# Forming two of the four weight sums of a seven-product matmul by an accumulating transfer instead of on VectorE

## The reference

```python
h2 = rmsnorm(x, norm2_g[l])                                        # (1, 256, 2048)
x = x + jnp.square(jax.nn.relu(h2 @ w_mlp_in[l])) @ w_mlp_out[l]   # 2048 -> 8192 -> 2048
```

## Time and profile before

| | us |
|---|---|
| median of three runs | 2813.29 |
| the three runs | 2812.1, 2817.95, 2813.29 |
| the profiled execution, its time | 2816.21 |
| its span (first to last instruction) | 2814.5 |
| TensorE busy | 2791.1 |
| VectorE busy | 2227.4 |
| ScalarE busy | 1489.3 |
| GpSimd busy | 2.0 |
| share of the 16 DMA engines taken by SyncE's queue | 68.8% |

### The profile page before, as it was taken

The page is one execution under the profiler, slowest core; times in us unless marked ns, Lnnn a source line. Parts: engine busy times, 40 slices in busy tenths (PEclk is TensorE's granted clock), DMA queues, the critical chain, the costliest instruction groups (busy, mean ns, idle before and its releaser), DMA issues.

```text
span 2814.5 us, 33866 instructions
## 1 busy us (share of the span) xinstructions
PE 2791.1 (99%) x13102; PEld 2300.4 (82%) x13102; DVE 2227.4 (79%) x2487; ACT 1489.3 (53%) x1674; POOL 2.0 (0%) x7
## 2 busy tenths in 40 slices
PE   9999999999999999999999999999999999999998
PEld 7888878888887888888888888888888788888887
DVE  6697855556778999999967678877667999999986
ACT  6644446544455555555556444444455555555654
POOL 0000000000000000000000000000000000000000
PEclk9999999999999999999999999999999999999999
DMA  9576656666866677767677767667676767677774
GB/s 313 160 222 201 204 160 211 195 195 198 257 210 212 219 235 243 245 212 239 223 243 218 223 199 215 200 206 224 209 219 208 243 215 239 219 242 226 246 233 166
DMA packets 371808, 615.42 MB, mean 219 GB/s; under 512 B 22976, under 2 KB 96320, under 8 KB 371008
## 3 DMA queue, kind: packets, MB, share of 16 engines
q1 hardware_dynamic: 371216, 612.94, 68.8%
q10 hardware_dynamic: 432, 0.32, 0.0%
HBM read 575.69 MB, written 2.10 MB: 205 GB/s over the span
## 4 chain that ended last, share of the span: by engine, by line
PE 83%; DVE 8%; DMA 5%; ACT 2%; issue 2%; SPq 1%; DVEq 0%; ACTq 0%
PE ACC L864 67%; PE TB L870 8%; PE ACC L870 6%; DVE WL L1609 2%; DMA RAW<-in_w_mlp_in_dram 2%; DMA RAW<-in_w_up_dram 2%; DMA RAW<-in_w_down_dram 1%; DVE FG L1622 1%; ACT WH L1136 1%; DVE FG L1624 1%; DVE FG L1626 1%; DVE X L2121 0%; DVE HT L2094 0%; SPq L758 0%; DVE TWL L1633 0%
## 5 line engine op out<-in xcount | busy, mean ns | idle before, releaser
L1136 ACT ACTIVATE WH<-RAW 128x1024 fp32r<-128x1024 f32 (+1 forms) x1023 | 1027.8, 1020 | 1016.4 <-PE ACC L864 619.1
L1609 DVE TENSOR_TENSOR WL<-RAW,WH 128x1024 fp32r<-128x1024 f32 (+1 forms) x1023 | 1185.6, 1172 | 405.5 <-ACT WH L1136 402.5
L864 PE MATMUL ACC<-WH,XTH 128*128 128x512 f32 (+1 forms) x1692 | 658.1, 389 | 0.4 <-DVE XTL L1683 0.4
L864 PE MATMUL ACC<-WL,XTH 128*128 128x512 f32 (+1 forms) x1692 | 655.1, 387 | 0.0
L864 PE MATMUL ACC<-WH,XTL 128*128 128x512 f32 (+1 forms) x1692 | 655.1, 387 | 0.0
L864 PEld LDWEIGHTS ACC<-WH,XTH 128*128 128x128 f32 x1692 | 317.8, 188 | 66.8 <-DVE XTL L1683 0.8
L864 PEld LDWEIGHTS ACC<-WH,XTL 128*128 128x128 f32 x1692 | 317.7, 188 | 65.1
L864 PEld LDWEIGHTS ACC<-WL,XTH 128*128 128x128 f32 x1692 | 317.8, 188 | 63.6
L864 PE MATMUL ACC<-WH,YAH 128*128 128x512 f32 x864 | 336.4, 389 | 0.0
L864 PE MATMUL ACC<-WL,YAH 128*128 128x512 f32 x864 | 336.1, 389 | 0.0
L864 PE MATMUL ACC<-WH,YAL 128*128 128x512 f32 x864 | 336.1, 389 | 0.0
(11 more groups left out here) (383 smaller groups left out, 3146.6 us busy)
## 6 DMA issues: line engine op xcount, KB each, us to landing
RAW<-in_w_in_dram SPq DMA_DIRECT2D x255, 512.0 KB, 4.5
RAW<-in_w_mlp_out_dram SPq DMA_DIRECT2D x128, 512.0 KB, 5.0
RAW<-in_w_down_dram SPq DMA_DIRECT2D x128, 512.0 KB, 5.1
RAW<-in_w_mlp_in_dram SPq DMA_DIRECT2D x116, 512.0 KB, 4.6
RAW<-in_w_up_dram SPq DMA_DIRECT2D x116, 512.0 KB, 4.5
RAW<-in_w_gate_dram SPq DMA_DIRECT2D x96, 512.0 KB, 4.5
YT<-HT SPq DMA_DIRECT2D x208, 128.0 KB, 3.2
RAW<-in_w_branch_dram SPq DMA_DIRECT2D x48, 512.0 KB, 4.1
```

The source lines that it names most:

```text
L864: ins = e.matmul(ACC[:, 2 * (b % 2) + half, 0:n], p[:, k, xs], q[:, t, 0:n], start=(k == 0 and m == 0), stop=(k == nk - 1 and m == 2))
L1136: e.activation(WH[u % NSPL][:, ts, 0:n], RAW[u % NRAW][:, ts, 0:n], ACT.Copy).then_inc(hi, 1)
L1609: e.tensor_tensor(l, r, h, ALU.subtract).then_inc(lo, 1)
```

## The change

For the quads made ahead (24 in the run), the first VectorE instruction of three (L1622, 128 x 1024: T1 and T3 at once) goes. Instead GpSimd issues one transfer with an add: it reads the two tiles of the pair's second block again from HBM (512 KB) and adds them to slots 0 and 2 of `FG`, where SyncE has just loaded the tiles of the first block's upper row and the second block's upper row. GpSimd waits for the load first (`ld_sum`), and VectorE now waits for the add (`add_sum`) and then makes T2 and T4 with one instruction of 512 columns each.

A transfer can add and not subtract, so all quads use sums with other signs: in `weight_sums` every `subtract` becomes `add`. To make up for it `x_sums` swaps operands and turns one add and one subtract round, and `product_sums` uses two `tensor_tensor` subtracts and two `scalar_tensor_tensor` instead of four `tensor_tensor` adds. The counts that `t_sum` reaches come from a table, since a quad made ahead now counts two and not three.

The positions change too. The sum of the first quad moves from h - 15 to h - 14, its high part from h - 14 to h - 13, its low part from h - 11 and h - 10 to h - 12 and h - 11. The second quad's load moves from unit h - 3 to h - 4, its sum from h - 6 to h - 5, its high part from h - 5 to h - 4, its low part from h - 4 and h - 3 to h - 3 and h - 2.

```diff
+    SUMMED = {}
+    for rec in sorted({rec for rec, m in SEVEN.values()}, key=lambda rec: rec.q):
+        SUMMED[rec.q] = SUMMED.get(rec.q - 1, 0) + (2 if rec.ahead else 3)
...
-            at("ahead_sum", h - 15)
-            at("ahead_hi", h - 14)
-            at("ahead_lo", h - 11, 2)
-            at("ahead_sum", h - 6)
-            at("ahead_hi", h - 5)
-            at("ahead_lo", h - 4, 2)
-            AHEAD_LOAD[h - 13], AHEAD_LOAD[h - 3] = AHEAD_OF[n, 0], AHEAD_OF[n, 1]
+            at("ahead_add", h - 16)
+            at("ahead_sum", h - 14)
+            at("ahead_hi", h - 13)
+            at("ahead_lo", h - 12, 2)
+            at("ahead_add", h - 8)
+            at("ahead_sum", h - 5)
+            at("ahead_hi", h - 4)
+            at("ahead_lo", h - 3, 2)
+            AHEAD_LOAD[h - 13], AHEAD_LOAD[h - 4] = AHEAD_OF[n, 0], AHEAD_OF[n, 1]
...
             if rec.ahead:
-                b11_12, b12_22, b21, b22 = tr[:, 0:4:2, :], tr[:, 2:4, :], tr[:, 1, :], tr[:, 3, :]
-                e.wait_ge(ld_sum, 32 * LOADED[rec.q])
+                b21, b22 = tr[:, 1, :], tr[:, 3, :]
+                e.wait_ge(add_sum, 16 * LOADED[rec.q])
...
-            e.tensor_tensor(tr[:, T1:T3 + 1:T3 - T1, :], b12_22, b11_12, ALU.subtract).then_inc(t_sum, 1)
-            e.wait_ge(t_sum, 3 * rec.q + 1)
-            e.tensor_tensor(tr[:, T2, :], b22, tr[:, T1, :], ALU.subtract).then_inc(t_sum, 1)
-            e.wait_ge(t_sum, 3 * rec.q + 2)
-            e.tensor_tensor(tr[:, T4, :], b21, tr[:, T2, :], ALU.subtract).then_inc(t_sum, 1)
+            if not rec.ahead:
+                e.tensor_tensor(tr[:, T1:T3 + 1:T3 - T1, :], b12_22, b11_12, ALU.add).then_inc(t_sum, 1)
+                e.wait_ge(t_sum, SUMMED[rec.q] - 2)
+            e.tensor_tensor(tr[:, T2, :], b22, tr[:, T1, :], ALU.add).then_inc(t_sum, 1)
+            e.wait_ge(t_sum, SUMMED[rec.q] - 1)
+            e.tensor_tensor(tr[:, T4, :], b21, tr[:, T2, :], ALU.add).then_inc(t_sum, 1)
...
-            e.tensor_tensor(sx[:, S_1], AX[:, :, 0, 1, :], AX[:, :, 1, 1, :], ALU.add).then_inc(xs, 1)
-            e.tensor_tensor(sx[:, S_3], sx[:, S_A], AX[:, :, 0, 1, :], ALU.subtract).then_inc(xs, 1)
+            e.tensor_tensor(sx[:, S_1], AX[:, :, 1, 1, :], AX[:, :, 0, 1, :], ALU.subtract).then_inc(xs, 1)
+            e.tensor_tensor(sx[:, S_3], AX[:, :, 0, 1, :], sx[:, S_A], ALU.subtract).then_inc(xs, 1)
...
-                e.tensor_tensor(h12, h11, acc_bank(b0, 1), ALU.add).then_inc(mid, 1)
+                e.tensor_tensor(h12, acc_bank(b0, 1), h11, ALU.subtract).then_inc(mid, 1)
                 e.wait_ge(mid, 2 * n + 1)
-                e.tensor_tensor(h21, h12, acc_bank(b0 + 1, 1), ALU.add).then_inc(acc[b0 % 2], 1)
+                e.scalar_tensor_tensor(out=h21, in0=h12, scalar=-1.0, in1=acc_bank(b0 + 1, 1), op0=ALU.mult, op1=ALU.subtract
+                                       ).then_inc(acc[b0 % 2], 1)
...
+        def sum_add():
+            for k, rec in enumerate(AHEAD_OF.values()):
+                w, _, c0, n = plan[PAIR[rec.u][1] + 1]
+                rows = w[2 * rec.i * P:(2 * rec.i + 2) * P, c0:c0 + n].rearrange("(g t j) n -> j (g t) n", g=4, t=2)
+                e.wait_ge(ld_sum, 32 * k + 32)
+                e.dma_start(TR[rec.buf[1]][:, 0:4:2, :], rows, accum_op=ALU.add).then_inc(add_sum, 16)
+                yield
+
+        tasks = {"gm_tril": gm_tril, "ahead_add": sum_add, "block1_end": pad}
```

More of the change, by code:

```diff
@@ L189, in build @@
     ld_x0 = [sem(f"ld_x0_{k}") for k in range(8)]
-    ld_sum = sem("ld_sum_tiles")
+    ld_sum, add_sum = sem("ld_sum_tiles"), sem("sum_tiles_added")
     ld_gb = [sem(f"ld_gate_bias{i}") for i in range(2)]
@@ L772, in _ @@
                 if u - NRAW in SEVEN and not SEVEN[u - NRAW][0].ahead:
-                    e.wait_ge(t_sum, 3 * SEVEN[u - NRAW][0].q + 3)
+                    e.wait_ge(t_sum, SUMMED[SEVEN[u - NRAW][0].q])
             if u == 0:
@@ L1140, in sums_high @@
             sums_free(e, rec)
-            e.wait_ge(t_sum, 3 * rec.q + 2)
+            e.wait_ge(t_sum, SUMMED[rec.q] - 1)
             e.activation(parts[0][:, T_PARTS[0], :], tr[:, T_PARTS[0], :], ACT.Copy).then_inc(t_hi, 1)
-            e.wait_ge(t_sum, 3 * rec.q + 3)
+            e.wait_ge(t_sum, SUMMED[rec.q])
             e.activation(parts[0][:, T_PARTS[1], :], tr[:, T_PARTS[1], :], ACT.Copy).then_inc(t_hi, 1)
@@ L2158, in x_sums @@
             e.wait_ge(xs, m + NI + 2)
-            e.tensor_tensor(sx[:, S_1], AX[:, :, 0, 1, :], AX[:, :, 1, 1, :], ALU.add).then_inc(xs, 1)
-            e.tensor_tensor(sx[:, S_3], sx[:, S_A], AX[:, :, 0, 1, :], ALU.subtract).then_inc(xs, 1)
+            e.tensor_tensor(sx[:, S_1], AX[:, :, 1, 1, :], AX[:, :, 0, 1, :], ALU.subtract).then_inc(xs, 1)
+            e.tensor_tensor(sx[:, S_3], AX[:, :, 0, 1, :], sx[:, S_A], ALU.subtract).then_inc(xs, 1)
             yield
             e.wait_ge(xs, m + NI + 3)
-            e.tensor_tensor(sx[:, S_2], sx[:, S_1], sx[:, S_A], ALU.subtract).then_inc(xs, 1)
+            e.tensor_tensor(sx[:, S_2], sx[:, S_1], sx[:, S_A], ALU.add).then_inc(xs, 1)
             yield
@@ L2185, in product_sums @@
                 e.wait_ge(mm, PAIR_END[n] + 1)
-                e.tensor_tensor(h12, h11, acc_bank(b0, 1), ALU.add).then_inc(mid, 1)
+                e.tensor_tensor(h12, acc_bank(b0, 1), h11, ALU.subtract).then_inc(mid, 1)
                 e.wait_ge(mid, 2 * n + 1)
-                e.tensor_tensor(h21, h12, acc_bank(b0 + 1, 1), ALU.add).then_inc(acc[b0 % 2], 1)
+                e.scalar_tensor_tensor(out=h21, in0=h12, scalar=-1.0, in1=acc_bank(b0 + 1, 1), op0=ALU.mult, op1=ALU.subtract
+                                       ).then_inc(acc[b0 % 2], 1)
                 yield
                 evicted(e, "h" + tag, j, 0)
-                e.tensor_tensor(h22, h21, acc_bank(b0 + 1, 0), ALU.add).then_inc(mid, 1)
+                e.scalar_tensor_tensor(out=h22, in0=h21, scalar=-1.0, in1=acc_bank(b0 + 1, 0), op0=ALU.mult, op1=ALU.subtract
+                                       ).then_inc(mid, 1)
                 e.wait_ge(mid, 2 * n + 2)
-                e.tensor_tensor(h12, h12, acc_bank(b0 + 1, 0), ALU.add).then_inc(acc[(b0 + 1) % 2], 1)
+                e.tensor_tensor(h12, h12, acc_bank(b0 + 1, 0), ALU.subtract).then_inc(acc[(b0 + 1) % 2], 1)
                 yield
@@ L2442, in pad @@
             yield
-        tasks = {"gm_tril": gm_tril, "block1_end": pad}
+        def sum_add():
[6 more added lines that the diff above has]
+        tasks = {"gm_tril": gm_tril, "ahead_add": sum_add, "block1_end": pad}
         run(e, stream, tasks)
```

## The result

The changed kernel takes 2846.26 us in the median of four runs (2843.32 to 2847.2), against 2814.23 for the kernel before on the same occasions: 1.0109 times as long, 95% interval 1.0093 to 1.0125, so +32 us. The forecast was 2820.1, range 2809 to 2842. Its direction was right, its size was not.

A forecast was written before the change was run, and what follows sets the result against it. TensorE was taken as the bound, busy 2791.1 of 2814.5 us. Later sums added 6.8 us (12 x 0.57), the adding transfer and changed signs nothing: 2813.3 + 6.8 = 2820.1 us, range 2809 to 2842.

The forecast's parts named there:

- At most 6.4 us can be won: TensorE's waits in the pairs, without each block's first pair: the most the change could win, 6.4 us or 0.23%.
- A delay of the cut of h - 1 reaches TensorE in full, through the load of h + 3 and the residual addition: Chain before unit h + 1: already late by 0.2 us, so any delay of VectorE's cut becomes TensorE waiting.
- The sums behind the residual addition cost 0.57 us per pair with two short instructions: Second quad's two remaining sums, now after that addition, make the cut of h - 1 late: 12 x 0.57 = 6.8 us.
- A: Time from the landing of the loads in FG to the landing of GpSimd's add; taken as 5.95 us.
- A is 5.95 us, a weight load and as many bytes again: GpSimd's add: weight load of 4.6 plus 1.35 us for the bytes reread from SBUF, just inside 6.1, costing nothing more.
- The bound of 10.3: Upper bound in us for the add's time, from the load of four times the bytes; 64 us more there.
- the point from which it costs, 6.1: Second quad: an add up to 6.1 us is free; each microsecond above reaches TensorE.
- The load that moves up is free: Second quad's load ahead of h - 4's: bytes before h - 3's load unchanged, so h - 3 still lands at 941.64.
- Crowding: Rival: the add pushes back weight loads of h - 3 to h - 1, 23 us in 12 pairs, 2837 us; chance 0.12.
- A slow add: Rival: add takes near 10.3 us and VectorE waits, 6.8 + 64 us, 2884 us; chance 0.06.

The follow-up runs named there:

- the copy: The changed kernel with GpSimd's adding transfer turned into a plain copy of the same rows to the same place: 2821.8 us, 1.0018 of the kernel before.
- the wide sum at the same place: The changed kernel's signs and positions without the adding transfer, VectorE making all three sums: 2846.9 us, 1.0108 of the kernel before.
- The spare tile: Second quad alone uses the add, into a separate 4 KB per partition tile loaded at h - 9, positions of before: 2809.9 us, 0.9980, fastest of all.
- the sums moved alone: No add, first quad at changed positions, second quad's sums and parts moved but its load before h - 3 as before: 2860.0 us, 1.0150.
- the add for second quads: The changed kernel with the adding transfer for second quads only, first quads made by VectorE at old positions: 2862.4 us, 1.0161.
- the sums still later: The changed kernel with the second quad's sums in h - 4, high part in h - 3, both low parts in h - 2: 2825.8 us, 1.0034.
- the load moved alone: No add, first quad at changed positions, second quad's load before h - 4 but its sums and parts at old positions: 2839.9 us, 1.0083.

## Why the prediction was wrong, point by point

- *At most 6.4 us can be won.* Nothing speaks against it: the best version found wins 6.3, with an interval of 3 to 8.
- *A delay of the cut of h - 1 reaches TensorE in full, through the load of h + 3 and the residual addition.* Right. All 12 pairs stop there, and in pair after pair the wait is the distance less 1.6 us (3.52 and 1.90 in the kernel after, 2.73 and 1.12 in the copy).
- *The sums behind the residual addition cost 0.57 us per pair with two short instructions.* Borne out as far as it can be: the copy, with A at 6.7 and 0.5 us of VectorE's wait in pair n = 1, gives 0.8 us of wait per pair, 0.5 more than the kernel before; the wide sum at the same place gives 1.8, 1.5 more. One reading in it was off without harm: unit h - 3 was copied at 940.58 and not at 941.64, so VectorE wanted the add at 944.04 and not at 945.0.
- *A is 5.95 us, a weight load and as many bytes again.* This is the step that failed. A is 7.7 us for the second quads in the median, and 8.9 in pair n = 1. A plain copy in the same place takes 6.4 in the median (6.7 in pair n = 1), so adding takes 1.3 us more (2.1 there), 0.4 of them in the issue. The bound of 10.3 held, and the point from which it costs, 6.1, was about right: 0.57 + 1.5 us of mean wait, 12 times, is 25 us, against 22.0 measured as standing. I took the value "just inside" the threshold, and the term was nil there and is 19 us at 7.7. The rows had a better one. The 4.6 in it is the median of the loads of `w_mlp_in` into `RAW` over the whole program, but the loads into `FG` have 6.5, and the prediction itself had given the load of this very quad 7.7 us, 931.2 to 938.9. With 6.5 + 1.35 = 7.85 us the same sum gives 6.8 + 12 x 1.75 = 28 us, 2841.
- *The clock.* Left out of the sum. The copy's stops, 0.8 us on average, left it at its upper level throughout the pairs; those of the kernel after, up to 2.1 us, cost 5.1 us of clock in all, after three of the twelve.
- *The load that moves up is free.* Wrong, hidden by an argument about bytes in front of h - 3: it puts unit h - 4 behind 1 MB, and with VectorE's three sums in their old place it costs 22 us. In the copy it did not show; that the removed instruction pays it back there is likely, but no run tells the two apart.
- *Crowding* fell. *A slow add* was the right rival, priced at its far bound alone (A of 10.3, 2884) and given 0.06, so the stretch between 6.1 and 10.3, in which it came out, had next to no chance. The page of the Trainium skill, "DMA: Bandwidth & Descriptors", section "Anatomy of one DMA", gave an estimate of 3.2 or 4.4 us; the 6.3 of the copy and the 7.7 of the add, measured with the 16 engines full, decide against using it here.
- Open: how A divides between the adding and the queue. The spare tile's adds go out at another place and still take 7.8 to 8.1 us from issue to landing, but the 16 engines are busy there too (share 0.82 to 1.00 while they run, against 0.90 to 1.08 in the kernel after). No run shows an add on idle engines.

## What to carry to other kernels

When a sum of terms has a wait with a threshold, find how far the unknown is from the threshold before taking its best value: an expected cost over its range (here 3.6 to 10.3, threshold 6.1, each value as likely) would have given some 17 us for this term where the best value gave none. Take the price of a transfer from the nearest transfer in the same stretch, not from the median of all. Work handed to a transfer is best asked for long before it is wanted, at a place where its buffer is free early: twelve adds with 20 us of room came out at -6 us, twenty-four with 6 us of room at +32, though the two kernels differ in more than the room. And where loads come just in time, moving one forward moves another back.

## What the runs showed of the hardware that was not expected

- A transfer from GpSimd with an add of 512 KB takes 7.7 to 7.9 us from issue to landing (medians; 6.6 to 9.8 in the single transfers) and 1.11 to 1.24 us of GpSimd; the same as a copy 6.3 us and 0.72 (one of 0.84); it needs 6528 packets for 24 transfers against 3456.
- TensorE's clock fell to its lower level after some stops of 1.8 to 2.1 us, and not after others of the same length, and stayed there about 3.4 us. Added up over the pairs, 5.1 us of clock were missing in the kernel after (3 stretches), 8.5 in the run with the sums moved alone (5), 10.2 with the add for second quads (6), and none in the kernel before, the copy, the sums still later and the spare tile, whose stops reach 1.7 us at most. With the load moved alone, stops up to 1.7 us, none was missing either.
